# Scan of a hybrid decoder block: the gated rows of seven of eight groups turned into columns by VectorE, with the decay products and both matrix products one slot sooner

## The chip, the cores and the metric

The kernel runs on one core of one Trainium2 chip. The metric is device microseconds of one execution, the lower the better. Before the change three runs gave 2051.84, 2053.12 and 2055.95 us, so the median is 2053.12 us.

## The reference, cut to what matters

The kernel computes one decoder layer for 256 tokens of width 2048, all in float32. A normed input is projected by one wide matrix. Two mixers work on it, sparse attention and a Mamba2 scan, their gated sum is projected again, and a squared-ReLU MLP follows. The change lies in the second mixer, which in the reference reads (conv, softplus and state recursion shortened):

```python
xbc = silu(conv(xbc) + conv_b); xs, bm, cm = split(xbc)       # xs: 64 heads of 64, in 8 groups
y = ssd_chunked(xs * dt, dt * a, bm, cm)                      # two chunks of 128 tokens
#   cb = cm @ bm.T; decay = exp(masked differences of cumsum(dt * a)); y_diag = (cb * decay) @ x
#   y_off = (cm @ state of chunk 0) * exp(cumsum);  y = y_diag + y_off
y = (y + ssm_d[:, None] * xs) * silu(z)
yg = y.reshape(B, S, 8, 512); yg = yg * rsqrt(mean(yg * yg, -1) + EPS)
o_ssm = yg.reshape(B, S, 4096) * ssm_norm_w
merged = sigmoid(gate_a) * (o_nsa @ w_proj_nsa) + sigmoid(gate_b) * (o_ssm @ w_proj_ssm)
```

So each of the eight groups gives 256 tokens by 512 channels of `yg`. The projection `o_ssm @ w_proj_ssm` needs these with the channels on the partitions, so the rows have to be turned.

## The kernel before

Every large product is made in three passes, because a float32 operand is kept as a high and a low part: high by high, low by high, high by low. The weights stream through a ring of four buffers of 128 x 2 x 512 numbers. For each buffer ScalarE copies the high part (`split_hi`, L260), VectorE subtracts it from the raw data (`split_lo`, L266), and TensorE multiplies (`mm_group`, L299 to L301): two tiles of the inner dimension, two row tiles of tokens, three passes, so 12 matmuls of 512 columns. That is one slot. Eight slots are a chunk, which fills two PSUM banks.

The order of the work is written out by hand. Each engine walks the slots in step (`slots` on ScalarE and VectorE, `mm_chunk` on TensorE), and between the slots it runs hooks, small pieces of the other work. At slot s ScalarE and VectorE first split the buffer of slot s + 3 (`LEAD`), and then run the hooks of slot s. TensorE multiplies slot s, then runs its hooks. All engines take their own queue strictly in order, so a hook that waits for a semaphore holds back all that is behind it on that engine. SyncE loads a buffer as soon as the low part of the group four before it has been made (it waits on `s_lo`).

The scan is spread over iterations of 16 slots (`scan_iteration`), in which two chunks of the input projection are multiplied: 512 columns of xBC and 512 columns of z. Beside the chunk of iteration i + 1, the hooks scan group i. An iteration without a scan comes first, four with groups 0 to 3 follow, then four plain chunks of the first half of `w_proj_ssm` (`C_PB1`), three iterations with groups 4 to 6, and group 7 beside the first two chunks of the second half of `w_proj_ssm` (`C_PB2`, with slots in the order of `PAIR` and its hooks moved by `last_hooks`).

In one such iteration, before the change:

- ScalarE slot 0 copies the conv output to token rows (`token_rows`, L1201). Slots 1 and 2 make the decay of both chunks (`scan_exp`, L1208, L1210). Slot 4 copies the state product out of PSUM (`scan_state`, L1214, signals `s_stc`). Slot 8 starts the conv of the next group (`conv`), slot 9 sums squares (L1219), slot 10 scales the rows by the rsqrt (`scan_norm`, L1224, signals `s_yn`), slot 12 splits the turned y (`scan_split`, L348) and takes the tanh of the conv (`conv_tanh`), and slot 15 takes the z chunk and its tanh (`take_z`, L1195).
- VectorE slot 0 takes `C B` products from PSUM and finishes the z gate in ZT (`scan_first`), slot 1 scales the inputs (`scan_inputs`, L1647, L1650), slots 3 and 4 multiply the decays by the C B products (`scan_w`, L1604, signals `s_w`), slot 6 and 8 read the chunk products (`scan_y0`, `scan_y1`). Slots 9 to 11 add the conv taps (`taps`, L1542), slot 12 ends the conv (`conv_out`), slot 13 turns the conv output by 32 x 32 blocks (`turn_rows`, L1656) and then makes the low part of the turned y (`scan_split`, L366), slot 15 takes the second half of the z chunk (`take`, L1302).
- TensorE runs `scan_cb` after slot 0, `scan_state` after slot 4 (L941), `scan_y0` after slot 6 (L945, waits for `s_stc` and for the decay product of chunk 0), `scan_y1` and the turn of the xBC rows after slot 8 (L957, L945, L334), and `scan_turn_y` after slot 12: eight transposes of 128 x 128 of Y into the banks X6 and X7 (L334).
- GpSimd (POOL) makes the rsqrt (L606 to L611), multiplies the skip term (L729), loads the rows of cumulative sums and issues the four DMAs that spread the conv blocks (`spread_rows`, L723).

In the merge and the MLP another way of turning is in use: `turn_blocks` (VectorE transposes by 32 x 32 blocks), `spread_blocks` (four DMAs from GpSimd which put the blocks in place in SBUF) and the splits `act_split_s` and `dve_split_s` from SBUF.

## Time and profile before

| | |
|---|---|
| median of three runs | 2053.12 us |
| the profiled execution, own time | 2053.77 us |
| its span | 2052.0 us |
| TensorE matmul busy | 2032.3 us (99%) |
| VectorE busy | 1344.0 us (66%) |
| ScalarE busy | 1024.0 us (50%) |
| GpSimd busy | 202.6 us (10%) |
| mean granted TensorE clock | 0.997 of full |
| scan iterations in the span | about 658 to 1210 us, with four plain chunks between |

The profiled execution took 2053.77 us, 1.8 us more than its span, which is the time around it. Shares of busy time are means over stages. Within the scan iterations VectorE and ScalarE have more to do than in the mean. A row of the timeline gives the start and length of an instruction, and in brackets how long its engine had been idle before it and what it was waiting for. Matmuls overlap in the rows, so the distance from start to start is what one of them costs.

### The profile page before, as it was taken

The page shows a single profiled execution, that of the slowest core. Times are in us where ns is not written, and L with a number is a line of the kernel's source. Part 1 is how long each engine was busy: PE and PEld are TensorE (multiplying, and loading weights), DVE is VectorE, ACT ScalarE, POOL GpSimd, SP SyncE. Part 2 cuts the span into 40 slices and gives each one's busy share as a digit, 9 for nine tenths or more (in the row PEclk, how much of TensorE's full clock was granted, in tenths as well). Part 3 has the DMA queues.
Part 4 walks back from the last instruction along what each step waited for, and adds up shares of the span by engine and source line. Part 5 has one row for each costly group of instructions (what it writes and reads, how often), then busy time and mean ns, then how long its engine had stood idle before and what let it go on. Part 6 is the DMA issues. An engine that isn't in the chain of part 4 may idle for free.

```text
span 2052.0 us, 26419 instructions
## 1 busy us (share of the span) xinstructions
PE 2032.3 (99%) x9394; PEld 1681.8 (82%) x9394; DVE 1344.0 (66%) x1623; ACT 1024.0 (50%) x1437; POOL 202.6 (10%) x362
## 2 busy tenths in 40 slices
PE   9999999999999999999999999999999999999997
PEld 7888888888888878888888888888888888888886
DVE  6755676676665677775677767666546656655664
ACT  5444545554543466664566644554434434434443
POOL 4000010101010011110011110100001000000000
PEclk9999999999999999999999999999999999999999
DMA  8756565656657666666666667766666666766664
GB/s 274 216 166 194 168 200 159 202 168 200 175 176 234 186 187 195 193 194 210 182 182 195 194 226 239 225 208 222 209 193 204 223 196 190 229 200 182 224 214 134
DMA packets 201765, 408.85 MB, mean 199 GB/s; under 512 B 14945, under 2 KB 15041, under 8 KB 200241
## 3 DMA queue, kind: packets, MB, share of 16 engines
q1 hardware_dynamic: 188656, 364.56, 57.4%
q0 software_dynamic: 12816, 42.34, 7.0%
q8 instruction: 74, 1.21, 0.2%
q14 instruction: 43, 0.34, 0.1%
q10 hardware_dynamic: 176, 0.40, 0.1%
HBM read 379.91 MB, written 2.16 MB: 186 GB/s over the span
## 4 chain that ended last, share of the span: by engine, by line
PE 90%; DVE 3%; issue 2%; ACT 2%; DMA 1%; DVEq 1%; ACTq 0%; POOL 0%; POOLq 0%; SPq 0%
PE acc L299 28%; PE acc L301 28%; PE acc L300 28%; DVE lo L266 1%; PE x L945 1%; PE tr L334 1%; PE x L885 1%; PE tr L902 1%; ACT hi L260 1%; DMA GA<-x 0%; ACT W L1208 0%; PE x L892 0%; PE x L817 0%; PE tr L904 0%; PE tr L907 0%
## 5 line engine op out<-in xcount | busy, mean ns | idle before, releaser
L266 DVE TENSOR_TENSOR lo<-raw,hi 128x1024 fp32r<-128x1024 f32 x688 | 835.7, 1229 | 505.5 <-ACT hi L260 499.8
L260 ACT ACTIVATE hi<-raw 128x1024 fp32r<-128x1024 f32 x688 | 717.9, 1056 | 614.1 <-PE acc L301 559.6
L299 PE MATMUL acc<-hi,LAh 128*128 128x512 f32 x1840 | 730.0, 397 | 2.2 <-DVE lo L266 2.1
L301 PE MATMUL acc<-hi,LAl 128*128 128x512 f32 x1840 | 717.3, 390 | 0.0
L300 PE MATMUL acc<-lo,LAh 128*128 128x512 f32 x1840 | 716.7, 390 | 0.0
L299 PEld LDWEIGHTS acc<-hi,LAh 128*128 128x128 f32 x1840 | 345.6, 188 | 78.9 <-DVE lo L266 6.2
L301 PEld LDWEIGHTS acc<-hi,LAl 128*128 128x128 f32 x1840 | 345.4, 188 | 72.5
L300 PEld LDWEIGHTS acc<-lo,LAh 128*128 128x128 f32 x1840 | 345.7, 188 | 71.2 <-issue 1.4
L299 PE MATMUL acc<-hi,LBh 128*128 128x512 f32 x896 | 350.6, 391 | 0.0
L300 PE MATMUL acc<-lo,LBh 128*128 128x512 f32 x896 | 349.2, 390 | 0.0
L301 PE MATMUL acc<-hi,LBl 128*128 128x512 f32 x896 | 349.1, 390 | 0.0
L300 PEld LDWEIGHTS acc<-lo,LBh 128*128 128x128 f32 x896 | 168.7, 188 | 35.2 <-issue 0.2
L301 PEld LDWEIGHTS acc<-hi,LBl 128*128 128x128 f32 x896 | 168.6, 188 | 35.2
L299 PEld LDWEIGHTS acc<-hi,LBh 128*128 128x128 f32 x896 | 168.7, 188 | 34.9 <-issue 0.2
L382 POOL DMA_DIRECT2D W<-TB x48 | 26.0, 560 | 491.8 <-DVE TB L373 491.8
L1542 DVE SCALAR_TENSOR_TENSOR XCT<-XCT,CWs 128x255 f32<-128x255 f32 (+2 forms) x144 | 59.8, 477 | 0.0
L382 POOL DMA_DIRECT2D XTOK<-W x48 | 26.0, 558 | 219.1 <-DVE W L373 219.1
L1023 ACT ACTIVATE XR<-acc,RSX 128x512 f32<-128x512 f32 x28 | 19.3, 690 | 54.7 <-PE acc L301 53.0
L1124 ACT ACTIVATE PB<-x,NM 128x256 f32<-128x256 f32 (+1 forms) x64 | 26.0, 418 | 35.8 <-DVE SCB L1500 25.6
L688 POOL DMA_DIRECT2D BCT<-BCT x36 | 19.6, 565 | 224.4 <-DVE BCT L1529 224.4
L1208 ACT ACTIVATE W<-W,NAs 128x128 f32<-128x128 f32 x128 | 39.0, 388 | 0.0
L729 POOL TENSOR_TENSOR XTOK<-XTOK,DBC 128x512 f32<-128x512 f32 x16 | 23.1, 1463 | 157.2 <-DVE Y L1650 157.2
(308 smaller groups left out, 1237.2 us busy)
## 6 DMA issues: line engine op xcount, KB each, us to landing
raw<-w_in SPq DMA_DIRECT2D x304, 512.0 KB, 4.0
raw<-w_up SPq DMA_DIRECT2D x128, 512.0 KB, 4.1
raw<-w_down SPq DMA_DIRECT2D x128, 512.0 KB, 4.8
raw<-w_proj_ssm SPq DMA_DIRECT2D x64, 512.0 KB, 4.2
raw<-w_proj_nsa SPq DMA_DIRECT2D x32, 512.0 KB, 4.4
raw<-w_out SPq DMA_DIRECT2D x32, 512.0 KB, 5.6
W<-acs_rows POOLq DMA_DIRECT2D x8, 1024.0 KB, 4.9
W<-TB POOLq DMA_DIRECT2D x48, 128.0 KB, 4.2
```

The source lines that it names most:

```text
L260: act.activation(hi[:, sl, :, :], raw[:, sl, :, :], ACT.Copy).then_inc(s_hi, 1)
L266: dve.tensor_tensor(lo[:, sl, :, :], raw[:, sl, :, :], hi[:, sl, :, :].bitcast(F32), ALU.subtract).then_inc(s_lo, 1)
L299: pe.matmul(o, xh, wh, start=(k == 0), stop=False)
L300: pe.matmul(o, xh, wl, start=False, stop=False)
L301: x = pe.matmul(o, xl, wh, start=False, stop=(k == KT - 1))
L334: x = pe.transpose((banks or TR)[b][:, (ct % 2) * S + t * P:(ct % 2) * S + (t + 1) * P], src[:, t, ct * P:(ct + 1) * P], identf[:, :])
L382: eng.dma_start(TSS[n % 2][:, S * a:S * (a + 1)], TBS[n % 2][32 * a:32 * (a + 1), :].rearrange("i (b n) -> i b n", b=4)).then_inc(s_sp[n % ...
L729: pool.tensor_tensor(heads8(XD[:, t, :]), heads8(XTOK[:, t, :]), DBC[:, 8 * g:8 * g + 8].unsqueeze(2).broadcast_to([P, 8, SH]), ALU.mult). ...
L885: pe.matmul(X6[:, :].rearrange("p (b k n) -> p k b n", b=2, k=2)[:, k, :, :], q1, KG[:, i, k, 0:2 * P].rearrange("p (b n) -> p b n", b=2), ...
L1124: act.activation(o, src, ACT.Exp, scale=SCALE, bias=NM[:, k:k + 1], accum_out=SUM[:, k:k + 1])
L1208: act.activation(W[:, h, c, :], W[:, h, c, :], ACT.Relu, bias=NAs[:, c, h:h + 1], scale=-1.0)
L1542: dve.scalar_tensor_tensor(XC[:, ct, k:S], TH[:, ct, 0:S - k], CWs[:, 3 - k, ct:ct + 1], XC[:, ct, k:S], ALU.mult, ALU.add)
```

## The change

The gated and normed rows of groups 0 to 6 are no longer transposed by TensorE. VectorE turns them by 32 x 32 blocks from Y into ZT, the buffer of the z gate (`turn_y`, slot 10, behind the taps of that slot). Four DMAs from GpSimd spread the blocks back into Y (`spread_y`), and the norm weights are staged behind them. ScalarE scales the four column tiles in place and copies the high part from SBUF (`split_y`, slot 14), and VectorE subtracts (`split_y`, slot 15, one instruction of 1024 in place of four of 256 from PSUM). Group 7 keeps the transposes of TensorE, after slot 10 in place of 9, with its splits in slot 10 on both engines.

The decay products move from VectorE's slots 3 and 4 to 2 and 3, the first chunk product and its reading from slot 6 to 5, the second from 8 to 7. The copy to token rows on ScalarE moves from slot 0 to slot 1. TensorE's `scan_cb` waits for the gated y of the group before instead of its split, and the products with `w_proj_ssm` that read groups 5 and 6 wait for their splits. In VectorE's iteration the `take` of slots 7 and 15 and the taps of slot 10 stand ahead of the scan's hooks.

```diff
@@ -222,7 +222,9 @@
         s_zt = sem("z_tanh_ready")
         s_yg = sem("gated_y_ready")
         s_yn = sem("normed_y_ready")
-        s_e3 = sem("y_transposed")
+        s_yb = sem("y_blocks_turned")
+        s_ysp = sem("y_blocks_spread")
+        s_e3 = sem("last_y_transposed")
         s_e3a = sem("y_read_by_act")
         s_e3d = sem("y_read_by_dve")
         s_hr = sem("residual_landed")
@@ -501,6 +503,9 @@
         ZT = sb("ZT", [P, 2, NC], c=post)
         TB = sb("TB", [P, 2 * NC], c=post)
         TS = W[:, 0:4, :, :].rearrange("p h c l -> p (h c l)")
+        TY = Y[:, :, :].rearrange("p t n -> p (t n)")
+        TZ = ZT[:, :, :].rearrange("p t n -> p (t n)")
+        TYV = TY.rearrange("p (a m j) -> p m a j", a=4, j=32)
         TSS = (TS, XTOK[:, :, :].rearrange("p t n -> p (t n)"))
         TBS = (TB[:, :], W[:, 4:8, :, :].rearrange("p h c l -> p (h c l)"))
         post.close()
@@ -516,7 +521,7 @@
 
         def last_hooks(hooks):
 
-            last = {6: 5, 8: 6, 9: 7, 10: 8, 12: 9, 13: 9}
+            last = {7: 6, 9: 7, 10: 8, 11: 10, 12: 10}
             return {last.get(s, s): h for s, h in hooks.items()}
 
         def heads4(x):
@@ -716,6 +721,13 @@
                 pool.dma_start(W[:, :, :, :].rearrange("p h c l -> p (h c l)"),
                                acs_rows[ds(8 * S * g, 8 * S)].partition_broadcast(P)).then_inc(s_row, 16)
 
+            def spread_y(g):
+
+                pool.wait_ge(s_yb, g + 1)
+                for a in range(4):
+                    pool.dma_start(TY[:, S * a:S * (a + 1)], TZ[32 * a:32 * (a + 1), :].rearrange("i (b n) -> i b n", b=4)).then_inc(s_ysp, 16)
+                pool.tensor_copy(NWs[:, :], COLS[:, 4 * g + CSN:4 * g + CSN + 4]).then_inc(s_pg, 1)
+
             def spread_rows(t):
 
                 pool.wait_ge(s_xb, t + 1)
@@ -740,12 +752,14 @@
                 stage_conv(m, 4 * t)
                 load_rows(t)
                 rms(2 + 2 * t, NC, RS[:, 0:2])
+                if t:
+                    spread_y(t - 1)
                 spread_rows(t)
-                stage_scan(t)
 
             for t in range(8):
                 scan_iteration(t, 4 + t)
             skip_term(7)
+            stage_scan(7)
             rms(18, NC, RS[:, 0:2])
             pool.wait_ge(s_ey, 8)
             for t in range(2):
@@ -927,7 +941,7 @@
 
 
             def scan_cb(g):
-                pe.wait_ge(s_e3d, g + 1)
+                pe.wait_ge(s_yg, g) if g else None
                 BTg, CTg = BCT[:, g, :], BCT[:, g + 8, :]
                 pe.transpose(X7[:, 2 * P:3 * P], BTg[:, 0:P], identf[:, :])
                 for c in range(2):
@@ -961,8 +975,8 @@
                 pe_turn(pe, None, Y, [(s_yn, g + 1)], banks=(X6, X7), sm=s_e3)
 
             def scan_hooks(g):
-                return {0: [lambda: scan_cb(g)], 4: [lambda: scan_state(g)], 6: [lambda: scan_y0(g)],
-                        8: [lambda: scan_y1(g)], 12: [lambda: scan_turn_y(g)]}
+                return {0: [lambda: scan_cb(g)], 4: [lambda: scan_state(g)], 5: [lambda: scan_y0(g)],
+                        7: [lambda: scan_y1(g)], 11: [lambda: scan_turn_y(g)] if g == 7 else []}
 
             def scan_iteration(C, par, e, g=None):
                 hooks = scan_hooks(g) if g is not None else {}
@@ -983,6 +997,8 @@
             for s, (c, j) in enumerate(PAIR):
                 if s == 6:
                     pe.wait_ge(s_acc, C_PB2)
+                if s in (0, 4):
+                    pe.wait_ge(s_e3d, 7 + s // 4)
                 if s == 12:
                     pe.wait_ge(s_e3d, 9)
                 mm_group(pe, 8 * C_PB2 + s, (C_PB2 + c) % 2, j, LBh, LBl)
@@ -1226,11 +1242,21 @@
 
             def scan_split(g, k0):
                 act.wait_ge(s_pg, g + 1)
-                act_split_t(act, g, LBh, k0, NWs, banks=(X6, X7), sm=s_e3, done=s_e3a)
+                act_split_t(act, 0, LBh, k0, NWs, banks=(X6, X7), sm=s_e3, done=s_e3a)
+
+            def split_y(g, k0):
+                act.wait_ge(s_pg, g + 1)
+                act.wait_ge(s_ysp, 64 * g + 64)
+                for ct in range(4):
+                    v = TYV[:, 2 * ct:2 * ct + 2, :, :]
+                    act.activation(v, v, ACT.Copy, scale=NWs[:, ct:ct + 1])
+                act.drain()
+                act.activation(tokens(LBh, k0), TYV, ACT.Copy).then_inc(s_e3a, 2)
 
             def scan_hooks(g, k0):
-                return {0: [lambda: token_rows(g)], 1: [lambda: scan_exp(g, 0)], 2: [lambda: scan_exp(g, 1)], 4: [lambda: scan_state(g)], 9: [lambda: scan_squares(g)],
-                        10: [lambda: scan_norm(g)], 12: [lambda: scan_split(g, k0)]}
+                return {1: [lambda: token_rows(g), lambda: scan_exp(g, 0)], 2: [lambda: scan_exp(g, 1)], 4: [lambda: scan_state(g)], 9: [lambda: scan_squares(g)],
+                        10: [lambda: scan_norm(g)], 11: [lambda: scan_split(g, k0)] if g == 7 else [],
+                        14: [lambda: split_y(g, k0)] if g < 7 else []}
 
             def scan_iteration(C, par, e, m, g=None, k0=None):
                 hk = scan_hooks(g, k0) if g is not None else {}
@@ -1606,7 +1632,19 @@
 
             def scan_split(g, k0):
                 dve.wait_ge(s_pg, g + 1)
-                dve_split_t(dve, g, LBh, LBl, k0, NWs, banks=(X6, X7), sa=s_e3a, done=s_e3d)
+                dve.wait_ge(s_e3a, 16)
+                dve_split_t(dve, 0, LBh, LBl, k0, NWs, banks=(X6, X7), sa=s_e3a, done=s_e3d)
+
+            def split_y(g, k0):
+                dve.wait_ge(s_e3a, 2 * g + 2)
+                dve.tensor_tensor(tokens(LBl, k0), TYV, tokens(LBh, k0).bitcast(F32), ALU.subtract).then_inc(s_e3d, 1)
+
+            def turn_y(g):
+                dve.wait_ge(s_yn, g + 1)
+                for t in range(2):
+                    x = dve.transpose(TZ.rearrange("p (b c t j) -> p t c b j", b=4, c=4, t=2)[:, t, :, :, :],
+                                      Y[:, t, :].rearrange("p (c i b) -> p c b i", c=4, b=4))
+                x.then_inc(s_yb, 1)
 
             def scan_first(g):
                 dve.wait_ge(s_cb, g + 1)
@@ -1637,8 +1675,10 @@
 
             def scan_hooks(g, k0):
                 return {0: [lambda: scan_first(g)], 1: [lambda: scan_inputs(g)],
-                        3: [lambda: scan_w(g, 0)], 4: [lambda: scan_w(g, 1)], 6: [lambda: scan_y0(g)], 8: [lambda: scan_y1(g)],
-                        13: [lambda: scan_split(g, k0)]}
+                        2: [lambda: scan_w(g, 0)], 3: [lambda: scan_w(g, 1)], 5: [lambda: scan_y0(g)], 7: [lambda: scan_y1(g)],
+                        10: [lambda: turn_y(g)] if g < 7 else [],
+                        12: [lambda: scan_split(g, k0)] if g == 7 else [],
+                        15: [lambda: split_y(g, k0)] if g < 7 else []}
 
             def scan_inputs(g):
 
@@ -1659,13 +1699,13 @@
 
             def scan_iteration(C, par, m, xa, g=None, k0=None):
                 hk = scan_hooks(g, k0) if g is not None else {}
-                hk[7] = hk.get(7, []) + [lambda: take(C, par, XR[:, 1, :], xa + 1)]
+                hk[7] = [lambda: take(C, par, XR[:, 1, :], xa + 1)] + hk.get(7, [])
                 hk[9] = [lambda: taps(m, 1)] + hk.get(9, [])
-                hk[10] = hk.get(10, []) + [lambda: taps(m, 2)]
+                hk[10] = [lambda: taps(m, 2)] + hk.get(10, [])
                 hk[11] = hk.get(11, []) + [lambda: taps(m, 3)]
-                hk[12] = [lambda: conv_out(m, XC[:, :, :])]
-                hk[13] = [lambda: turn_rows(m)] + hk.get(13, [])
-                hk[15] = [lambda: take(C + 1, (par + 1) % 2, ZR[:, 1, :], xa + 2)]
+                hk[12] = [lambda: conv_out(m, XC[:, :, :])] + hk.get(12, [])
+                hk[13] = [lambda: turn_rows(m)]
+                hk[15] = [lambda: take(C + 1, (par + 1) % 2, ZR[:, 1, :], xa + 2)] + hk.get(15, [])
                 slots(dve, split_lo, C, 16, hk)
 
             def add_gated(groups, par, cols, o, T):
@@ -1695,8 +1735,8 @@
                 turn_blocks(dve, n, MG[n % 2])
 
             hk = last_hooks(scan_hooks(7, 12))
-            hk[13] = hk.get(13, []) + [lambda: merge(0, 8 * C_PB2 + 14)]
-            hk[14] = hk.get(14, []) + [lambda: turn_merged(0)]
+            hk[13] = [lambda: merge(0, 8 * C_PB2 + 14)]
+            hk[14] = [lambda: turn_merged(0)]
             hk[15] = [lambda: merge(1, 8 * C_PB2 + 16)]
             slots(dve, split_lo, C_PB2, 16, hk)
             slots(dve, split_lo, C_PB2 + 2, 8, {0: [lambda: turn_merged(1)], 3: [lambda: dve_split_s(dve, 0, E_PB2, LAh, LAl, 0)],
```

## Rows read from the trace of the kernel before

**Rows 1.** The page: busy time, share and instructions by engine; the chain that ended last.

```profile
PE 2032.3 (99%) x9394; PEld 1681.8 (82%) x9394; DVE 1344.0 (66%) x1623; ACT 1024.0 (50%) x1437; POOL 202.6 (10%) x362
...
PE 90%; DVE 3%; issue 2%; ACT 2%; DMA 1%; DVEq 1%; ACTq 0%; POOL 0%; POOLq 0%; SPq 0%
```

**Rows 2.** Waits of PE, whole span: total us, times, longest.

```profile
PE x L945 <- DVE W L1604: 1.2, 1, 1.2
PE x L334 <- ACTq L1225: 0.8, 1, 0.8
```

**Rows 3.** Waits, 710 to 766 us (the iteration of group 0).

```profile
PE acc L299 <- DVE lo L266: 1.2, 2, 0.7
```

**Rows 4.** Timeline of PE, group 2: start us, length, operation.

```profile
818.03 0.27 PE L932 MATMUL x<-identf,BCT 128*128 128x128 f32 x1
...
833.12 0.39 PE L299 MATMUL acc<-hi,LAh 128*128 128x512 f32 x1
...
835.85 1.90 PE L945 MATMUL x<-XDT,W 128*128 128x64 f32 x16
...
846.51 0.47 PE L299 MATMUL acc<-hi,LAh 128*128 128x512 f32 x1
...
857.52 1.03 PE L334 MATMUL x<-identf,Y 128*128 128x128 f32 x8
858.31 0.48 PE L299 MATMUL acc<-hi,LAh 128*128 128x512 f32 x1
858.62 0.40 PE L300 MATMUL acc<-lo,LAh 128*128 128x512 f32 x1
...
869.29 0.27 PE L932 MATMUL x<-identf,BCT 128*128 128x128 f32 x1
```

**Rows 5.** Timeline of DVE, group 2, slots 9 to 15.

```profile
851.33 1.23 DVE L266 TENSOR_TENSOR lo<-raw,hi 128x1024 fp32r<-128x1024 f32 x1 [2.05 <-ACT hi L260]
...
857.40 1.23 DVE L266 TENSOR_TENSOR lo<-raw,hi 128x1024 fp32r<-128x1024 f32 x1 [0.39 <-ACT hi L260]
...
863.90 2.08 DVE L1656 STREAM_TRANSPOSE TB<-XCT 128x512 f32<-128x512 f32 x2
865.90 1.62 DVE L366 SCALAR_TENSOR_TENSOR LBl<-x,NWs,LBh 128x256 fp32r<-128x256 f32 x4
...
869.71 0.75 DVE L1302 TENSOR_SCALAR XR<-acc,RSX 128x512 f32<-128x512 f32 x1
```

**Rows 6.** Timeline of ACT, group 2.

```profile
818.80 1.06 ACT L1195 ACTIVATE ZT<-XR 128x1024 f32<-128x1024 f32 x1 [2.61 <-DVE XR L1302]
...
832.50 0.58 ACT L1214 ACTIVATE XCT<-x 128x512 f32<-128x512 f32 x1
...
861.23 1.99 ACT L260 ACTIVATE hi<-raw 128x1024 fp32r<-128x1024 f32 x2
```

**Rows 7.** Lines by form of ACT: busy us, mean ns, idle before.

```profile
L400 ACT ACTIVATE LBh<-W,COLS 128x256 fp32r<-128x256 f32 x8 | 3.4, 493 | 0.0
```

**Rows 8.** Timeline of POOL, group 2: the four issues that spread blocks.

```profile
866.29 2.26 POOL L723 DMA_DIRECT2D XCT<-TB  x4 [11.56 <-DVE TB L1656]
```

**Rows 9.** Source line L723, spreads in the scan.

```profile
DMA to landing us min/median/max: 2.5/2.8/5.6
```

**Rows 10.** Source line L382, spreads in merge and MLP.

```profile
DMA to landing us min/median/max: 2.4/4.2/7.2
```

**Rows 11.** Timeline of ACT, group 0.

```profile
718.05 1.15 ACT L1201 ACTIVATE XTOK<-XCT 128x512 f32<-128x512 f32 x2 [2.64 <-DMA XCT<-TB]
```

**Rows 12.** Timelines of ACT and PE, group 7.

```profile
1176.62 0.58 ACT L1214 ACTIVATE XCT<-x 128x512 f32<-128x512 f32 x1
...
1178.38 2.09 PE L945 MATMUL x<-XDT,W 128*128 128x64 f32 x16 [1.25 <-DVE W L1604]
...
1180.80 0.63 PE L300 MATMUL acc<-lo,LBh 128*128 128x512 f32 x1
```

**Rows 13.** Stretch in group 7: busy us (x) of PE, PEld, DVE, ACT, POOL; PEclk, DMA, GB/s.

```profile
1180.00:1182.00 2.00, 2.00 (x8) 1.70 (x7) 2.00 (x3) 0.00 (x0) 0.00 (x0) 0.52 0.59 194
```

## The prediction

> **What bounds the kernel now.** I read the page first, for the busy shares [rows 1]. TensorE matmuls fill 2032.3 of 2052.0 us and 90% of the chain that ended last, so an instruction taken off TensorE is worth its full length unless a wait takes its place. I then read TensorE's waits [rows 2, 3]: in the scan there are only 1.2 us behind low parts in group 0, 1.2 us behind a decay product and 0.8 us behind the normed rows, both in group 7. So there is little to win from waits, and the question is how near the next ones are. For that I read the timelines of one steady iteration, group 2, engine by engine [rows 4 to 6]. The reader is to see two things there.
>
> First, what the turned rows cost TensorE: the eight transposes start at 857.52, the next matmul at 858.31, and its successor 0.31 us later, where a usual step is one twelfth of a slot. A slot is 835.85 - 833.12 = 2.73 us, so a step is 0.23. The price is 0.79 + 0.08 = 0.87 us per group [rows 4].
>
> Second, a loop that runs through all engines and is as long as TensorE's own work. Its origin is the end of the turn of the xBC rows, 846.51. From there the conv goes through ScalarE to VectorE, whose first low part after it starts at 851.33, 4.82 us on. VectorE then runs the taps, the conv's end, the block transposes and the split of the turned y nearly without a gap, and takes the z rows at 869.71 [rows 5]. I call that distance X: 23.20 us. In the iteration shown ScalarE's tanh follows the take by 0.78 us (it waits for it), and its queue (token rows, two decays, four high parts) brings it to the copy of the state, which ends at 833.08: 14.28 us after the tanh began [rows 6]. So the state copy ends X + 15.06 after the origin. The group that TensorE multiplies in slot 6 starts at 833.12 [rows 4], so slot 5 ends there. The state copy is done 0.04 us before. Today nothing waits for it, since the first chunk product comes a slot later. After the change that product stands exactly behind slot 5.
>
> **The change part by part.** The sum is made against the profiled execution, 2053.77 us, which lies 0.65 above the median.
>
> *Transposes off TensorE.* Seven groups at 0.87 us: -6.1 us if nothing else moves.
>
> *VectorE's chain.* It loses the split, whose row is 1.62 us long and overlaps the next by some 0.08, so 1.54 from start to start, and gains two block transposes before the low part at 857.40, 2.00 us as in slot 13 (863.90 to 865.90) [rows 5]. In front of that low part VectorE idled 0.39 us, which the transposes fill; their drain costs some 0.1. The subtraction of 1024 elements, 1.23 us as a low part is, comes behind the take and so outside X. X becomes 23.20 - 1.54 + 2.00 - 0.39 + 0.1 = 23.4, or 0.15 longer. At the same time TensorE would reach the end of slot 5 0.87 us sooner. The state copy, ending 0.15 later, is then late by 0.87 + 0.15 - 0.04 = 1.0 us, and TensorE waits before the first chunk product. From that product on all follows in series back to the origin (the product, slots 6 and 7, the second products, slot 8, the turn), so the wait is lost whole. Per iteration that is -0.87 + 1.0 = +0.1 instead of -0.87. Keeping the product in slot 6 would not avoid it: the low part of slot 6 is made from the same ScalarE queue. Of the seven intervals between groups, six close this loop. The one from group 3 to 4 has four plain chunks in it and pays in full. Gain there 0.9; the other six give back 6 x 1.0 = 6.1 (ends: 0, if ScalarE's queue finds slack that I overlook, and 6 x 1.5).
>
> *ScalarE's split.* Four scalings of 256 at 0.49 [rows 7], about 0.4 each when back to back, a drain and one copy of 1024, about 1.0 as a high part (861.23: two in 1.99 [rows 6]): 2.8 us in place of 1.57 of the same slots' reads from PSUM. It stands before the high part of slot 18, which VectorE wants at about 21.8 after the origin, against a split that can begin at 17.9. So 17.9 + 2.8 + 1.0 = 21.7: no slack at all, and each microsecond that the DMAs are late goes into X. The block transposes end at about 12.2 (up to 12.6); issue starts 0.3 later and the last of four is issued after 1.7 of its 2.26 us [rows 8]; landing takes 2.8 us in the median, at most 5.6, in this stage [rows 9], and 4.2 in the median in the later ones [rows 10]. That gives 17.0, 18.4 or 19.9, so a wait of 0, 0.5 or 2.0. SyncE's next loads go out just behind the transposes, so I take the middle. The copy to token rows has the same question one step on: its blocks are ready 1.7 later than now and the copy, one high part later in the queue, wants them 0.9 later; median landing covers it, the 7.6 us of group 0 (end of the transposes at about 710.5 to 718.05 [rows 11]) would cost 1.5. For both together I take +0.4 per closed loop, 2.4 in all (ends 0 and 12).
>
> *GpSimd.* Four more issues, 2.26 us, in an idle time of 11.56 [rows 8]: nothing. The norm weights' copy now stands behind them and ahead of the conv's spread, which comes 8 us later: nothing. If it ran into the spread it would cost up to 1.3 us of landing. The row load of the decays goes out with the second products and so one slot sooner, with no reader before the next iteration: 0.
>
> *Decay products sooner, token rows later.* VectorE has idle time in these slots, and the decays' exponentials are ready; 0, up to 0.7 if GpSimd's skip term slows them.
>
> *Group 0.* The two waits for low parts, 1.2 us [rows 3], go, because token rows wait for the DMA with one high part already made. A wait for the state copy replaces them, about 0.7: -0.5 (ends -1.2 and +1).
>
> *Group 7.* The chunk product started at 1178.38, 1.25 us late for its decay product, which now comes a slot sooner; the state copy ended at 1177.20 [rows 12]. Gain 1.2. After that wait the granted clock was 0.52 in 1180 to 1182 [rows 13], the 1.2 GHz level, and matmul steps there are 0.43 us (1180.80 and its neighbours) where they are 0.23 elsewhere: some 1.5 us lost. That goes if the wait goes. The turn's wait of 0.8 [rows 2] goes too, but the last two groups of its chunk now wait for the split, 3.4 us after the turn against one slot of 2.73: 0.7. Together -2.8.
>
> *The clock.* Each closed loop now holds a wait of 1.0 to 1.5 us in the very place where one of 1.25 brought the clock down. I count one such fall, +1.5 (ends 0 and 6 x 1.5 = 9).
>
> Sum: -6.1 + 6.1 + 2.4 - 0.5 - 2.8 + 1.5 = +0.6, so 2054.4 in the profiled execution's terms and **2053.7** beside the median.
>
> The Trainium skill (VectorE: DVE Perf Modes, section Rules for kernel authors) advises TensorE for a 128 x 128 turn where the result may go to PSUM, and gives TensorE 390 ns for one in bf16 (section The three transpose paths). The row has 0.87 us for eight in float32, a fourth of that. By the page's figure, an estimate, seven groups would free 21.8 us; the row decides.
>
> **The rivals.**
>
> *A. The saving is paid out.* The loop is looser than I have it (the low part behind the taps, say, or the exponentials run ahead) and TensorE waits only now and then. For it: TensorE waits for nothing in groups 1 to 6 today, so its slack is read from ends of rows, not from a wait. Against it: 0.04 us in the row. Time: -6.1 - 0.5 - 2.8 = -9.4, and with half a microsecond of waits in each of three loops -7.9: 2044 to 2046. If half of it comes true, 2049. Chance of this side 0.25.
>
> *B. The spread lands late, slower.* The place is ScalarE's slot 14. With a landing of 5.6 us as at worst [rows 9], or 7.6 from the end of the transposes as in group 0 [rows 11], ScalarE stands 2.0 us before the split, the z take and the tanh come as much later, and TensorE waits 3.0 instead of 1.0 for the state copy in six loops. That is 6 x 2.0 - 2.4 = +9.6 on the forecast, less if three loops only: +5. With two more falls of the clock, 3 more: 2058 to 2066. It decides from a landing of about 3.7 us on. For it: the same kind of spread exposes ScalarE in the MLP, with a median of 4.2 [rows 10]. Against it: in steady scan groups the conv's spread lands in 2.8. Chance 0.30.
>
> The Trainium skill (SBUF — State Buffer, section SBUF: two separate sides) warns that GpSimd's DMA descriptors starve while VectorE holds the shared port pair in its two-port modes. The four issues of group 2 ran beside VectorE's work in 2.26 us, so no such blocking shows there; if it came, it would be on this rival's side.
>
> *C. It does not do what it says.* If VectorE waited for the normed rows in slot 10 (they come at about 9.8, the taps end at 10.5), transposes would begin late, by 0.3 at most. That would leave the forecast.
>
> **How the numbers follow.** Forecast 0.45, with its own range 2050 to 2057; A 0.25; B 0.30. About 0.2%, 4.1 us, is what a measurement of this kernel tells from no change, so faster is below 2049.0 and slower above 2057.2. A lies mostly below, B mostly above: faster 0.25, same 0.45, slower 0.30. The range reaches from half of A to most of B: 2047 to 2061.
>
> **What would show it.** In the changed profile: 56 fewer transposes into x (8 left); TensorE's first chunk product waiting about 1 us for ScalarE's copy of the state in groups 1, 2, 3, 5, 6 and 7, and not in 4; iterations of about 51.3 to 52 us between scan_cb starts, where rows 4 have 51.26 (869.29 - 818.03); the z take about 23.4 after the turn of xBC; a clock of 0.5 in a stretch or two. I am wrong if iterations last 50.4 (A), or if ScalarE's wait for the spread exceeds 1.5 us in most groups (B).

## The result and the profile after

The changed kernel takes 2064.43 us (median of 6 runs, 2062.1 to 2065.47) against 2052.96 us (6 runs, 2051.84 to 2055.97) on the same chip: ratio 1.0053, 95% interval 1.0043 to 1.0064. It is 11.5 us slower. The forecast was 2053.7 with a range to 2061, so it was wrong. The profiled execution after has a span of 2062.4 us, where the one before had 2052.0: the 10.4 us below are worked out between these two.

The page after, busy time by engine and the chain that ended last, to be read beside [rows 1]:

```profile
PE 2034.8 (99%) x9338; PEld 1672.1 (81%) x9338; DVE 1360.7 (66%) x1616; ACT 1031.2 (50%) x1444; POOL 222.5 (11%) x390
...
PE 83%; issue 5%; ACT 4%; DVE 3%; DMA 1%; ACTq 1%; POOL 1%; POOLq 1%; DVEq 1%
```

TensorE has 56 instructions fewer, as the change says, but holds 83% of the chain instead of 90%. Other engines have come into it. The waits of TensorE over the whole span, where [rows 2] had 1.2 and 0.8 us in the scan:

```profile
PE x L959 <- ACT XCT L1230: 6.1, 6, 1.3
PE acc L301 <- DVE lo L268: 6.0, 17, 1.2
```

The first line is the wait that the prediction named (first chunk product for the copy of the state, in six groups, 1.0 us each). The second is a wait for low parts, which the prediction did not have. Before, it stood in the scan in group 0 alone (1.2 us, [rows 3]); now 4.2 us of it lie between 750 and 1260 us, in 13 waits. Its source is seen in the timelines of group 2. First VectorE, where [rows 5] had the split of y between the block transposes and the next low part:

```profile
860.11 2.11 DVE L1645 STREAM_TRANSPOSE ZT<-Y 128x512 f32<-128x512 f32 x2 [0.49 <-ACTq L1241]
862.14 1.18 DVE L268 TENSOR_TENSOR lo<-raw,hi 128x1024 fp32r<-128x1024 f32 x1
...
868.96 2.07 DVE L1696 STREAM_TRANSPOSE TB<-XCT 128x512 f32<-128x512 f32 x2
870.95 1.18 DVE L268 TENSOR_TENSOR lo<-raw,hi 128x1024 fp32r<-128x1024 f32 x1
873.32 1.23 DVE L268 TENSOR_TENSOR lo<-raw,hi 128x1024 fp32r<-128x1024 f32 x1 [1.19 <-ACT hi L262]
874.47 0.74 DVE L1328 TENSOR_SCALAR XR<-acc,RSX 128x512 f32<-128x512 f32 x1
```

The turn of the y rows begins 0.49 us late for the normed rows, and the take of the z rows comes after an idle 1.19 us behind a high part of ScalarE. ScalarE in the same stretch, beside [rows 6]:

```profile
869.50 1.71 ACT L1252 ACTIVATE Y<-Y,NWs 128x256 f32<-128x256 f32 x4 [1.58 <-DMA Y<-ZT]
871.28 1.06 ACT L1254 ACTIVATE LBh<-Y 128x1024 fp32r<-128x1024 f32 x1
872.25 1.04 ACT L262 ACTIVATE hi<-raw 128x1024 fp32r<-128x1024 f32 x1
...
878.55 1.15 ACT L1217 ACTIVATE XTOK<-XCT 128x512 f32<-128x512 f32 x2 [0.35 <-DMA XCT<-TB]
```

ScalarE stands twice in one loop: 1.58 us for the spread of y (1.2 to 1.6 us in each of the seven groups, 9.6 us in all), then, although this has already made it late, 0.35 us for the spread of the conv rows. For the conv rows it stands in two of the closed loops only; in the others it is late enough by itself. What the two spreads took from issue to landing, y's first, then the conv's, where [rows 9] had 2.5/2.8/5.6:

```profile
DMA to landing us min/median/max: 2.5/4.2/5.3
```

```profile
DMA to landing us min/median/max: 2.4/4.3/5.6
```

Why 4.3 and not 2.8 shows when GpSimd's issues are laid beside SyncE's raw loads. Group 2, after, GpSimd and then SyncE:

```profile
862.52 2.27 POOL L728 DMA_DIRECT2D Y<-ZT  x4 [3.89 <-DVE ZT L1645]
...
871.33 2.18 POOL L735 DMA_DIRECT2D XCT<-TB  x4 [6.35 <-DVE TB L1696]
```

```profile
863.49 0.37 SPq L249 DMA_DIRECT2D raw<-w_in  x1
866.75 0.37 SPq L249 DMA_DIRECT2D raw<-w_in  x1
869.03 0.37 SPq L249 DMA_DIRECT2D raw<-w_in  x1
872.30 0.37 SPq L249 DMA_DIRECT2D raw<-w_in  x1
```

And SyncE before, in the same group:

```profile
863.98 0.37 SPq L247 DMA_DIRECT2D raw<-w_in  x1
868.82 0.37 SPq L247 DMA_DIRECT2D raw<-w_in  x1
```

Each low part of VectorE frees a buffer, and SyncE issues the next load at its end. Before, the conv's spread was issued from 866.29 to 868.55 [rows 8], with no raw load issued between 863.98 and 868.82: VectorE was busy with the split of y, 1.6 us, and made no low part. After, both spreads have a raw load issued into them, 0.97 us after the first issue in each case. The same is seen before the change in the first spread of the scan, which has no split of y behind its turn: it is issued from 710.77, a raw load at 711.74, and its four DMAs land in 2.6, 4.3, 4.5 and 5.6 us.

Read as a loop from one end of the turn of the xBC rows to the next, as in the prediction (us after that end, the loop that holds the products of group 2; worked out from the timelines of each kernel; "lands" is the median landing of one DMA of the conv's spread over the whole scan; one fall of the clock lies in the loop of e2):

```
                     conv rows  z rows  token rows  state copy  loop   lands
                     turned     taken   begin       ends
before                 19.07    22.81     25.49       37.85     51.27   2.8
after                  21.14    24.48     28.54       39.95     53.56   4.3
e2 no spread of y      20.71    22.87     28.04       39.46     54.69   4.4
e5 products alone      19.04    22.77     25.54       37.93     51.52   2.7
e6 no block turn       20.37    22.54     27.69       39.10     52.70   4.4
e7 block turn alone    20.94    24.64     27.35       39.71     53.11   2.8
e8 turn behind rows    19.07    23.79     27.43       38.84     52.45   2.7
e10 split behind take  19.06    21.23     26.39       38.77     52.19   4.3
e11 ends, take sooner  19.06    21.66     25.48       37.86     51.28   2.8
```

The 10.4 us in the profile come together so: until the turn in group 0's iteration, -1.65 (742.16 against 743.81; 0.3 of it lies ahead of that iteration, where nothing was changed and the profiles differ by up to 0.4); five loops between turns +2.12, +2.29, +4.24, +1.93 and +2.08, of which 1.7 is a fall of the clock in the third; the long stretch from group 3 to 4 +0.86; from the turn in group 7's iteration to the end -1.47, which is +2.0 for the state copy of the sixth loop and -3.5 for the rest. The loops are the loss.

### The profile page after: what moved, and what is told of

It is laid out like the page before. It is cut to its first block, busy times and chain, and to the rows that moved or that the text cites. A ratio compares the mean times of both kernels' runs of the same rounds, so it can differ in the third digit from the quotient of the medians.

```text
span 2062.4 us, 26336 instructions
## 1 busy us (share of the span) xinstructions
PE 2034.8 (99%) x9338; PEld 1672.1 (81%) x9338; DVE 1360.7 (66%) x1616; ACT 1031.2 (50%) x1444; POOL 222.5 (11%) x390
## 4 chain that ended last, share of the span: by engine, by line
PE 83%; issue 5%; ACT 4%; DVE 3%; DMA 1%; ACTq 1%; POOL 1%; POOLq 1%; DVEq 1%
PE acc L301 26%; PE acc L303 25%; PE acc L302 25%; ACT W L1224 1%; ACT hi L262 1%; PE x L959 1%; DVE lo L268 1%; DMA XCT<-TB 1%; DMA Y<-ZT 1%; PE x L899 1%; PE tr L336 1%; ACTq L1225 1%; PE tr L916 1%; DVE ZT L1645 1%; POOLq L616 0%
## 5 line engine op out<-in xcount | busy, mean ns | idle before, releaser
L959 PEld LDWEIGHTS x<-XDT,W 128*128 128x128 f32 x256 | 31.1, 195 | 13.0 <-ACT XCT L1230 9.1
L741 POOL TENSOR_TENSOR XTOK<-XTOK,DBC 128x512 f32<-128x512 f32 x16 | 23.2, 1465 | 162.7 <-DVE Y L1690 162.7
```

What stands on the lines that cost most here:

```text
L741: pool.tensor_tensor(heads8(XD[:, t, :]), heads8(XTOK[:, t, :]), DBC[:, 8 * g:8 * g + 8].unsqueeze(2).broadcast_to([P, 8, SH]), ALU.mult). ...
L959: x = pe.matmul(X7[:, h * SH:(h + 1) * SH], W[:, h, c, :], XDT[:, c, h * SH:(h + 1) * SH], start=True, stop=True)
```

## The experiments

Theory L, on record with the first four, was that the landing of y's spread sets the loop. The rival S was that the shifted products do it, and the rival V that VectorE's two block transposes do, 2 us per group. All ratios are against the kernel before, run on the same chip.

**e1: the products back.**

```diff
-2: scan_w(g, 0), 3: scan_w(g, 1), 5: scan_y0(g), 7: scan_y1(g)
+3: scan_w(g, 0), 4: scan_w(g, 1), 6: scan_y0(g), 8: scan_y1(g)    # groups 0 to 6
```

> The changed kernel with the decay products and both chunk products of groups 0 to 6 back in the slots that they had before (3, 4, 6, 8). Theory L (the landing of the spread blocks holds ScalarE in slot 14, so the z take and all of ScalarE's queue behind it come late): the low part of slot 6 comes out of the same queue and is late as well, so the wait only changes its name; within 1.5 us of the changed kernel, 2063 to 2066. Rival S (the sooner products run into the state copy, and that is what costs): the waits of 0.9 to 1.3 us in six groups go, 2057 to 2059.

Measured 2062.41 us, ratio 1.0043 [1.0027, 1.006]; loop 53.44. The time stays (0.6 below L's range; its profile has no fall of the clock, where the changed kernel's has one, worth 1.7), the wait only changes its name. TensorE's waits in e1:

```profile
PE acc L301 <- DVE lo L268: 10.4, 26, 1.1
...
PE x L959 <- ACT XCT L1230: 1.0, 1, 1.0
```

S falls.

**e2: no spread of y.** VectorE still turns the rows, GpSimd issues nothing for them, ScalarE splits y unspread rows.

```diff
-for a in range(4): pool.dma_start(TY[...], TZ[...]).then_inc(s_ysp, 16)
-act.wait_ge(s_ysp, 64 * g + 64)
```

> The changed kernel without the four DMAs that spread the blocks of y (left out for groups 0 to 6: the split reads rows that were not turned); the block transposes, scalings and splits stay. Theory L: ScalarE does not stand in slot 14, the z take of VectorE comes 1.3 to 1.5 us sooner after the turn of xBC in six loops, so 8 us less than the changed kernel: 2055 to 2058. Rival S, and rival V (VectorE's two block transposes, 2 us per group, are what costs): no change, 2063 to 2066.

Measured 2066.25 us, ratio 1.0058 [1.004, 1.0075]. Theory L fell as the whole account. A part of it holds: in its three loops without a fall of the clock e2 is 0.4 to 0.9 us a loop shorter than the changed kernel, whose own fall is left out. The time hides this, because e2's profile has two falls, 5.1 us in all, against one of 1.7. The take came at 22.87, as the prediction's X had it or better, and yet the token rows came at 28.04. What held them in e2 is one line of ScalarE's waits from 700 to 1260 us:

```profile
ACT XTOK L1215 <- DMA XCT<-TB: 10.6, 7, 2.3
```

With y's landing gone, the conv's landing stands behind it, 7.3 us from the end of the turn to the reader, and holds ScalarE 1.5 us per group.

**e3 and e4: ScalarE's split later**, behind the high part that VectorE wants (e3), and behind the take (e4).

```diff
-14: [lambda: split_y(g, k0)]
+15: [lambda: split_y(g, k0)]        # e3: ahead of take_z; e4: between its take and its tanh
```

> The changed kernel with ScalarE's split of y in slot 15, behind the high part of slot 18 and ahead of the z take, in place of slot 14. Same work, same DMAs. Theory L: one high part of 1.0 us fits into the wait for the landing, and VectorE's low part of slot 18 is no longer late; about 1 to 1.3 us per closed loop, 6 to 8 us less than the changed kernel: 2056 to 2059. Rivals S and V: no change, 2063 to 2066.

> As the one before, but the split of y stands between ScalarE's half of the z take and the tanh of z, where ScalarE waits for VectorE's half anyway (1.4 us in the changed kernel, 2.6 before). Theory L: the take no longer waits for the landing; the tanh does, from the other side: it can begin when the split ends, about 23.5 to 24.5 us after the turn of xBC. 2055 to 2059, near the one before. Rivals S and V: no change, 2063 to 2066.

Measured 2067.36, ratio 1.007 [1.0053, 1.0087], and 2069.15, ratio 1.0084 [1.0068, 1.0101]. Both miss. VectorE takes z at 23.5 and 23.3, 1 us sooner than after the change, and the token rows still begin at 28.4 and 28.0 (waits for the conv's spread 8.8 and 10.7 us). Both profiles hold falls of the clock worth 3.4 us, 1.7 more than the changed kernel's. So two landings end within half a microsecond of each other, and hiding one shows the other.

New theory, T: what comes ahead of the turn of the conv rows (the block transposes, 2.0 us) delays both the take and the conv's spread; the split that went from behind it opened SyncE's queue to a raw load in the middle of the spread; and the loop has no slack for either.

**e5: the products alone**, in the kernel before.

```diff
-3: scan_w(g, 0), 4: scan_w(g, 1), 6: scan_y0(g), 8: scan_y1(g)
+2: scan_w(g, 0), 3: scan_w(g, 1), 5: scan_y0(g), 7: scan_y1(g)    # groups 0 to 6; slot 7's take ahead of it
```

> The kernel before, with the decay products and both products of groups 0 to 6 one slot sooner and nothing else. Theory T (the loop of each group is longer by the transposes' 2.0 us ahead of the conv rows' turn, and by the two landings behind it; the shifted products only give back what the missing PE transposes took): without the turning and its spread, the waits stay those of the kernel before; the end of the turn of the xBC rows to the next one stays 51.3 to 51.7 us, at most 0.3 more by waits for the decay products. 2052 to 2055. Rival S (the shift costs by itself, about 0.9 us a loop in waits at the first product): 2057 to 2060, waits of TensorE at the first product of 0.8 us and more.

Measured 2052.95, ratio 1.0007 [0.9997, 1.0016]; loop 51.52. No difference that can be told.

**e6: no block transposes.** What is spread and split is not y turned.

```diff
-x = dve.transpose(TZ..., Y[:, t, :]...)      # two of them
+dve.drain().then_inc(s_yb, 1)
```

> The changed kernel without VectorE's two block transposes of the gated rows (the rows that are spread and split are not the turned ones); the spread, its split and all slots stay. Theory T: the conv rows' turn ends 19.0 us after the end of the turn of the xBC rows instead of 21.2, both landings come 2 us sooner, token rows at about 26.3 instead of 28.3, state copy 38 to 38.6, the loop 51.3 to 52. 2050 to 2054. Rival (Y's spread on GpSimd's queue costs by itself, whatever VectorE's time): at least 2060.

Measured 2059.34, ratio 1.0047 [1.0031, 1.0062]. Only part of the loss goes. The conv rows turn at 20.37, not at 19.0, though nothing stands before them. The reason is on GpSimd. The power for the norm in this kernel, and the same step in the kernel before:

```profile
801.30 1.66 POOL L615 TENSOR_TENSOR RS<-VV,mhalf 128x2 f32<-128x2 f32 x1
```

```profile
802.28 0.75 POOL L610 TENSOR_TENSOR RS<-VV,mhalf 128x2 f32<-128x2 f32 x1
```

With the gaps ahead of it the norm is 1.3 us later, and VectorE's chain with it. And the conv's spread lands in 4.4, which in this kernel holds ScalarE 8.7 us in six waits. The time lies between the two ranges.

e6 also tells what a spread's landing hangs on, because its y rows are spread seven times under nearly the same work. Here are the first two, with the raw load of each, and VectorE's low part within the second:

```profile
753.34 2.27 POOL L728 DMA_DIRECT2D Y<-ZT  x4 [3.16 <-DVEq L1644]
754.51 0.37 SPq L249 DMA_DIRECT2D raw<-w_in  x1
...
804.75 2.25 POOL L728 DMA_DIRECT2D Y<-ZT  x4 [1.80 <-DVEq L1644]
805.62 1.23 DVE L268 TENSOR_TENSOR lo<-raw,hi 128x1024 fp32r<-128x1024 f32 x1 [1.68 <-ACT hi L262]
807.01 0.37 SPq L249 DMA_DIRECT2D raw<-w_in  x1
```

With the raw load at 1.17 us the second and third DMA land in 4.1 and 4.5 us, with it at 2.26 in 2.7 and 2.7 (2.7 to 2.8 in the five groups behind, too). VectorE makes a low part beside the fast one shown too, so VectorE's low part is not what slows a spread.

**e7: the block transposes alone**, in the kernel before; nobody reads them.

```diff
+10: dve.wait_ge(s_yn, g + 1); dve.transpose(ZT..., Y[:, t, :]...)   # two of them, groups 0 to 6, behind the taps
```

> The kernel before, with two block transposes of the same size in VectorE's slot 10 of groups 0 to 6, whose output nobody reads. Theory T: the conv rows' turn ends about 21.0 us after the turn of the xBC rows instead of 19.1; the split of y is still behind it, so the landing stays short (about 6.4 us), token rows at 27.4 instead of 25.7, the loop 52.8 to 53.3 instead of 51.5. 2060 to 2065. Rival (only the landings count, the transposes' 2 us lie in slack): 2052 to 2055.

Measured 2065.87, ratio 1.0069 [1.0052, 1.0085]; loop 53.11. A loss as large as the change's, with TensorE's transposes still in place, no second spread and the conv's landing at 2.8. In this kernel the split is still behind the turn, so VectorE has 2 us more to do; in the changed kernel it has only half a microsecond more. So e7 shows that the loop has no slack, and not by which way the changed kernel comes to be late. VectorE carries the 2 us through to the take:

```profile
815.59 2.08 DVE L1664 STREAM_TRANSPOSE TB<-XCT 128x512 f32<-128x512 f32 x2
817.57 1.64 DVE L366 SCALAR_TENSOR_TENSOR LBl<-x,NWs,LBh 128x256 fp32r<-128x256 f32 x4
819.10 2.37 DVE L266 TENSOR_TENSOR lo<-raw,hi 128x1024 fp32r<-128x1024 f32 x2
821.37 0.76 DVE L1302 TENSOR_SCALAR XR<-acc,RSX 128x512 f32<-128x512 f32 x1
```

**e8: no spread of y, block transposes behind the turn of the conv rows** (on other data, output unused).

```diff
-10: turn_y(g)
+13: turn_rows(m); two dve.transpose(XDT[:, 0, :]..., XDT[:, 1, :]...)
```

> The changed kernel without the four DMAs that spread the turned y rows (as in the run without them), and VectorE's two block transposes put behind the turn of the conv rows instead of ahead of it (on other data of the same size, output unused). Theory T: the conv rows turn at 19.0 us, VectorE's 2 us behind them keep the next raw load back as the split of y did in the kernel before, so that a DMA of the conv rows' spread lands in 2.8 to 3.5 us (median) again instead of 4.3; token rows at 25.5 to 26.5, the loop 51.3 to 52. 2050 to 2055. If only the place of the transposes counts and not the gap: the median stays at 4.3 us, token rows at 26.3 to 27, 2053 to 2057. If neither does: 2061 to 2066, as without the spread.

Measured 2056.59, ratio 1.0021 [1.0011, 1.0031]. The landing is 2.7 again, against 4.4 in e2, which differs only in where VectorE's 2 us stand (and in their data). The two profiled spans are 8.8 us apart, but 5.1 of it are e2's falls of the clock; e8 has none. SyncE issued no load from 812.10 to 817.97 around this issue of the spread:

```profile
814.45 2.27 POOL L733 DMA_DIRECT2D XCT<-TB  x4 [8.96 <-DVE TB L1694]
```

The token rows came later than I expected, 27.43: no landing holds them there, they follow the take at 23.79 by 3.65, not 2.7, because in the changed kernel they stand one high part later in ScalarE's queue. That costs the state copy nothing (from the take to its end it is 15.05 in e8, 15.04 before). What is left of the loss, 1.2 us in this loop, is mostly the take, 1.0 later than before: a pause of 0.2 and the transposes' 2.3 us stand behind the turn, where the split took 1.5.

**e9: the two ends only**, in the kernel before.

```diff
-3: scan_w(g, 0), 4: scan_w(g, 1)
+2: scan_w(g, 0), 3: scan_w(g, 1)                  # group 7 only
-0: token_rows(g)
+1: token_rows(g), ahead of scan_exp(g, 0)         # group 0 only
```

> The kernel before with two edits at the ends of the scan and none in the six closed loops: group 7's decay products one slot sooner, group 0's token rows behind the first high part of slot 1. Theory T: group 0 gives 1.0 to 1.3 us (from its first product of C and B to the end of the turn of the next rows 28.9 instead of 30.2), group 7 gives 1.2 us of wait and, if the clock stays up, 0.7 to 1.7 more; loops 1 to 6 stay 51.3 to 51.7. 2049 to 2051. Rival (what is won at the ends is taken up by the next wait for the raw loads or ScalarE): 2051.5 to 2053.5, no different from before.

Measured 2050.24, ratio 0.9986 [0.9977, 0.9995]. Group 0 gives 1.2 us in its own loop, from turn to turn (50.9 against 52.1), group 7 its wait, and the clock stays at full speed there.

**e10: VectorE's split behind the take**, in the kernel before.

```diff
-13: [lambda: scan_split(g, k0)]
+15: take(C + 1, ...), then scan_split(g, k0)       # groups 0 to 6
```

> The kernel before, with VectorE's split of y put behind the take of the gated columns instead of between the turn of the conv rows and the low part of slot 14. Theory T: the gap in which the conv rows' spread ran is gone, a DMA of it lands in about 4.3 us (median) instead of 2.8; token rows at 26.3 to 26.6 after the turn of the xBC rows instead of 25.5 although the take comes 1.6 us sooner, the loop 52.0 to 52.5: 2056 to 2060 (with a little more for the first product of C and B, which now waits for the split up to 0.9 us). Rival (the raw load does not slow the spread; the chain over the take sets the loop): token rows at 23.9 to 25.0, the loop 50 to 51, 2044 to 2051.

Measured 2060.54, ratio 1.0033 [1.0021, 1.0045]. The take is 1.6 us sooner, the token rows come 0.9 us later, and the loop is 0.9 us longer (the clock fell in group 7 here too, 3.4 us against 1.7 before). A raw load is again issued into the spread, 0.96 us after its first issue. ScalarE waits for the spread, which lands in 4.3:

```profile
815.89 0.37 SPq L247 DMA_DIRECT2D raw<-w_in  x1
...
821.95 1.16 ACT L1201 ACTIVATE XTOK<-XCT 128x512 f32<-128x512 f32 x2 [2.39 <-DMA XCT<-TB]
```

```profile
DMA to landing us min/median/max: 2.5/4.3/6.0
```

So the landing follows the gap in the raw loads here too, with no work added. The longer loop is another matter, because the edit makes a second thing late. TensorE's waits in e10, from 700 to 1260 us:

```profile
PE x L932 <- DVE LBl L366: 4.3, 6, 1.0
```

The first product of C and B waits for the split, which now stands behind the take: 0.57 to 1.0 us in each of six loops. TensorE never waits for the state copy. So e10 does not show what the slower landing costs by itself.

**e11: e9 with VectorE's take one low part sooner.**

```diff
-hk[15] = [lambda: take(C + 1, (par + 1) % 2, ZR[:, 1, :], xa + 2)]
+hk[14] = [lambda: take(C + 1, (par + 1) % 2, ZR[:, 1, :], xa + 2)]
```

> The kernel with the two edits at the ends, and VectorE's take of the gated columns one low part sooner (between the low parts of slots 14 and 15) in every scan iteration. The chain take, tanh, token rows, state copy then ends 1.1 us sooner in each loop. If TensorE is full in the kernel before (no gap over 0.4 us between its matmuls in a loop of 51.27 us), the loop stays 51.2 to 51.4 and the time 2049 to 2052, as without this edit; that is theory T, in which the chain had only just no slack and TensorE's own work set the loop. If the chain over the take set the loop: 50.2 to 50.6 a loop, 2043 to 2047.

Measured 2048.89, ratio 0.9979 [0.997, 0.9988]: the fastest version here, 0.2% below the kernel before. Its distance to e9 (2050.24) is inside both intervals. The loops are 51.26 to 51.28 in all five between turns. But in three of them the state copy ends where it did or at most 0.2 sooner, because the conv's landing, which nobody had waited for in these loops before, now holds the token rows. From 700 to 1260 us:

```profile
ACT XTOK L1201 <- DMA XCT<-TB: 5.7, 6, 1.7
```

In the other two the state copy ends 0.9 and 1.1 sooner than before. One of them was 51.3 before and stays so. The other was 51.7 before, with its state copy 0.4 later than in the rest, and comes down to 51.26 and no further. TensorE's waits in e11, same stretch:

```profile
PE x L334 <- ACTq L1225: 0.8, 1, 0.8
```

So 51.27 is TensorE's own work, and the chain over VectorE and ScalarE ended exactly with it in the kernel before: below, nothing is won (two loops of e11); above, each microsecond counts (e7: state copy +1.86, loop +1.84; and that one loop of the kernel before, +0.4 and +0.4).

Theory T's times held in e5 and e9 and within 0.1 us in e11. They were too low by 0.9 us in e7, 1.6 in e8, 0.5 in e10 and 5.3 in e6, where GpSimd's later norm was not foreseen.

## Why the prediction was wrong

**The bound and the loop: right.** TensorE full, the loop through all engines, the copy of the state 0.04 us before its reader: e7 and e11 show it. That the product's slot does not matter: right (e1, e5).

**VectorE's chain: right in size.** X was put at 23.4, from 23.2 in the loop that the prediction read (22.8 in most others). Without y's spread it was 22.87 to 23.23 (e2). It rested on exchanging 1.54 us of split for 2.00 us of transposes. The sum is right, and so is what the prediction says of the place: the split stood behind the turn of the conv rows and the transposes stand ahead of it, so the take hardly moves while the conv's spread starts later, 1.7 us by the forecast, 1.6 (e2) to 2.1 (after) measured.

**The step that failed: ScalarE's split and the landings, +0.4 us per closed loop.** I took a wait between none and 2.0 for y's spread, took the middle, and said for the conv's that "median landing covers it". The conv's landing was taken from [rows 9], which hold for a stretch without a raw load that the same change removes. Measured: y's blocks ready at 19.5 and 20.2 us after the origin in groups 1 and 2, where the prediction had 17.0, 18.4 or 19.9, so 1.4 us of wait per group; the conv's 4.3 instead of 2.8, so 7.3 to 7.4 us from the turn to its reader, with the token rows at 28.5; a take at the forecast's 23.4 + 0.4, and the 3.65 of e8 behind it, give 27.45. The state copy ended 1.8 to 2.5 later than before, where the prediction implies 0.6. In us per loop: -0.87 + 1.4 = +0.5 was forecast, +2.2 came on average (the sixth read from its state copy, the fall of the clock left out). Over six loops that is 9.7 us, and the forecast's sum (+0.6) and the 10.4 of the profile are 9.8 apart; the other terms miss by -1.2, -0.7, +0.2 and +1.8 and happen to cancel. e7 has 1.8 a loop without any new landing, and e2 1.4 to 1.8 with the conv's alone (53.2, 53.4 and 52.8 in three loops without a fall of the clock, against 51.4, 51.7 and 51.3); they do not add, they are parallel paths of nearly one length. This is why removing or moving y's landing (e2, e3, e4) gave back a fraction or nothing.

**Rival B: the right side, half of the mechanism.** It put the loss in slot 14 behind y's landing and had 2058 to 2066. The landing of 3.7 us from which it was to decide was passed. But its other sign, a wait of ScalarE above 1.5 us in most groups, was not: two of seven. TensorE's wait for the state copy stayed at 1.0 us, where B had 3.0. And e2, without that landing, had loops only 0.4 to 0.9 us shorter, so B as written does not explain the time.

The Trainium skill (DMA: Bandwidth & Descriptors, section Queues, rings and completion order) says that each DMA engine takes turns between the queues that have work for it, a packet at a time. By this rule a raw load issued into a spread takes turns with it. The trace agrees: 4.3 against 2.8 us, with the first DMA of each four, issued ahead of the load, at 2.4 to 3.3 either way. It does not show the turns themselves. And a raw load issued earlier does not slow the spread so: before, in group 2, the one issued 2.3 us ahead of it took 4.9 us to land and so was still on its way. It was the rule to weigh, with the question which loads the change lets run.

**GpSimd, "nothing": wrong by a little.** Its issues took the 2.2 us expected, with or without VectorE busy beside them. But the norm's power took 1.66 instead of 0.75 in six of seven groups, and the turn of y began 0.49 us late.

**Group 0: underrated, -0.5 forecast, -1.35 measured** in its own loop from turn to turn (50.75 against 52.10), the other 0.3 of the -1.65 being ahead of it. e5, with the products sooner, has 52.1, e9, with the token rows behind the high part, 50.9: the token rows' place gives 1.2 us of it, the products nothing.

**Group 7: -2.8 forecast, -3.5 measured. The clock: right.** One fall of 1.5 was counted, one of 1.7 came, in place of the one in group 7. That it was just one is luck: e1 had none, e2 and e3 two, e4 one of twice the length. The stretch behind the state copy's wait in group 3:

```profile
890.03 2.67 PE L959 MATMUL x<-XDT,W 128*128 128x64 f32 x16 [1.33 <-ACT XCT L1230]
```

```profile
890.00:892.00 2.00, 1.97 (x14) 1.98 (x15) 2.00 (x3) 1.86 (x2) 0.00 (x0) 0.79 0.47 85
892.00:894.00 2.00, 2.00 (x8) 1.71 (x8) 2.00 (x4) 0.00 (x0) 0.00 (x0) 0.50 0.80 217
894.00:896.00 2.00, 2.00 (x9) 1.65 (x8) 1.01 (x1) 0.00 (x0) 0.00 (x0) 0.86 0.92 310
```

The last three figures are the granted clock, the DMA share and GB/s: half speed for some 3 us after the wait, the 1.2 GHz level.

**The stretch from group 3 to 4: -0.9 forecast, +0.86 measured.** It is 138.3 us before, 137.6 in e2, 137.5 in e6, 139.3 in e7, and 139.1 in e9, which changes nothing there. This term stays open.

Also open: why the power takes 1.66 us. The five kernels with the second spread in GpSimd's program have it (after, e3, e4 and e6 in six groups, e1 in five); before, e2, e5 and e7 to e11 do not, except in group 7, which has 1.64 in all of them; no run separates the program's order from the DMAs' traffic. And a version that keeps TensorE free of the transposes with the chain as short as before was not found. Moving the split of y into the next iteration was not tried, for want of a buffer.

## What to carry to other kernels

- When a step goes from one engine to another, ask for each wait on the loop what it is ahead of now: 2 us taken from behind a transfer's start and put ahead of it leave the engine's sum as it was and delay the transfer by nearly all of it (1.6 us in e2).
- A transfer's landing time is measured beside the traffic that the old order let through. An engine step that looks idle for the transfer may be what holds the big loads back.
- Before removing work from the bound engine, move one step of the other chain by a known amount (e7, e11): it tells whether there is slack below the bound. Look in the trace whether the chain's end moved, since another wait can take its place, as the conv's landing did in e11.

## What was not expected of the hardware

- Four DMAs of 128 KB from SBUF to SBUF: 2.7 to 2.8 us median landing when no raw load is issued during them, 4.0 to 4.4 when one is. Each of the thirteen kernels fits; the first spread of the conv rows has a raw load in it in all of them, and lands as slowly in all. The spread of y shows it too: 4.2 after the change; 2.8 in e6, where it is issued from 804.75 to 807.00 and the next raw load at 807.01.
- GpSimd's power on 128x2 elements: 0.75 us in some programs and groups and 1.66 in others, the same line and shape; the pause ahead of it 0.60 or 0.93 us.
- A wait of 1.33 us of TensorE, followed by 64-column matmuls, was followed by half the clock in group 3 after the change, one of 1.26 us in group 2 was not. The length of the wait does not decide it: 1.59 us in group 7 of e2 and 1.96 us in group 7 of e7 had no fall behind them. One fall cost 1.7 us, worked out from the granted clock in stretches of 2 us.
